# The first attention's output units move into the dilated attention's blocks and are merged there with their gate

## The reference, cut to what matters

```python
proj = rmsnorm(x, g_mix) @ w_in           # q, k, v of both attentions, gate_pre
gates = sigmoid(gate_pre + b_gate)
g_sb, g_dl = gates[..., :1024], gates[..., 1024:]
y_sb = merge_heads(stick_breaking_attention(q_sb, k_sb, v_sb)) @ w_sb_out   # 512 -> 1024
y_dl = merge_heads(dilated_window_attention(q_dl, k_dl, v_dl)) @ w_dil_out  # 256 -> 1024
x = x + (g_sb * y_sb + g_dl * y_dl) @ w_o
```

## Time and profile before

| | us |
|---|---|
| median of 3 runs | 1140.44 (1138.16 to 1141.69) |
| profiled execution | 1136.11 |
| its span, first to last instruction | 1134.3 |
| TensorE busy in the span | 1102.1 (97%), weight load 942.2 (83%) |
| VectorE, ScalarE busy | 769.7 (68%), 540.7 (48%) |
| mean granted TensorE clock | 0.995 of 2.4 GHz |

### The profile page before, as it was taken

One profiled execution on the slowest core, in us unless ns is written; L12 is line 12 of the kernel. 1 busy time (PEld: TensorE's weight loads), 2 busy tenths in 40 slices (PEclk: granted clock), 3 DMA queues, 4 the chain that ended last, 5 costly groups with the idle time before them and its releaser, 6 DMA issues.

```text
span 1134.3 us, 15599 instructions
## 1 busy us (share of the span) xinstructions
PE 1102.1 (97%) x6039; PEld 942.2 (83%) x6039; DVE 769.7 (68%) x1080; ACT 540.7 (48%) x867; POOL 0.2 (0%) x4
## 2 busy tenths in 40 slices
PE   7989999999999999999999999999999999999996
PEld 5888899988998778877677788888898899989985
DVE  6876378745878778677666555568774578637864
ACT  6554155523553466666656433334553355514641
POOL 0000000000000000000000000000000000000000
PEclk9999999999999999999999999999999999999998
DMA  8223233332323212111110133433233233323221
GB/s 285 97 75 113 74 112 112 112 93 93 103 70 125 93 38 72 41 56 50 42 58 29 37 98 95 140 104 93 75 112 112 77 110 111 94 93 112 82 68 75
DMA packets 32904, 102.99 MB, mean 91 GB/s; under 512 B 4160, under 2 KB 5568, under 8 KB 32832
## 3 DMA queue, kind: packets, MB, share of 16 engines
q1 hardware_dynamic: 32832, 102.01, 28.8%
HBM read 99.90 MB, written 2.10 MB: 90 GB/s over the span
## 4 chain that ended last, share of the span: by engine, by line
PE 84%; DVE 8%; ACT 4%; issue 3%; DMA 1%; SPq 0%; DVEq 0%; ACTq 0%
PE acc_pair L1175 24%; PE acc_pair L1177 24%; PE acc_pair L1176 24%; PE pair_bank L1175 2%; PE pair_bank L1176 2%; PE pair_bank L1177 2%; DVE w_lo L758 1%; PE bank L1175 1%; PE bank L1177 1%; PE bank L1176 1%; ACT rope L628 1%; ACT w_hi L471 1%; PE bank L1183 1%; DVE rstd L783 1%; PE bank L1185 1%
## 5 line engine op out<-in xcount | busy, mean ns | idle before, releaser
L1175 PE MATMUL acc_pair<-xg_hi,w_hi 128*128 128x512 f32 (+1 forms) x693 | 266.0, 384 | 7.3 <-DVE w_lo L990 7.3
L1176 PE MATMUL acc_pair<-xg_lo,w_hi 128*128 128x512 f32 (+1 forms) x693 | 260.3, 376 | 0.0
L1177 PE MATMUL acc_pair<-xg_hi,w_lo 128*128 128x512 f32 (+1 forms) x693 | 259.8, 375 | 0.0
L471 ACT ACTIVATE w_hi<-w_raw 128x1024 fp32r<-128x1024 f32 (+2 forms) x159 | 153.5, 976 | 148.8 <-PE acc_pair L1177 148.6
L758 DVE TENSOR_TENSOR w_lo<-w_raw,w_hi 128x1024 fp32r<-128x1024 f32 (+2 forms) x159 | 178.5, 1125 | 46.7 <-ACT w_hi L471 45.3
L1175 PEld LDWEIGHTS acc_pair<-xg_hi,w_hi 128*128 128x128 f32 x693 | 131.2, 189 | 30.7 <-issue 8.0
L1177 PEld LDWEIGHTS acc_pair<-xg_hi,w_lo 128*128 128x128 f32 x693 | 130.8, 189 | 24.6
L1176 PEld LDWEIGHTS acc_pair<-xg_lo,w_hi 128*128 128x128 f32 x693 | 131.4, 190 | 19.9 <-issue 0.7
L1177 PE MATMUL acc_pair<-hid_hi,w_lo 128*128 128x512 f32 x352 | 138.8, 394 | 0.0
L1176 PE MATMUL acc_pair<-hid_lo,w_hi 128*128 128x512 f32 x352 | 138.2, 393 | 0.0
L1175 PE MATMUL acc_pair<-hid_hi,w_hi 128*128 128x512 f32 x352 | 136.9, 389 | 0.0
(11 more groups left out here) (217 smaller groups left out, 2057.6 us busy)
## 6 DMA issues: line engine op xcount, KB each, us to landing
w_raw<-in_w13b SPq DMA_DIRECT2D x44, 512.0 KB, 3.6
w_raw<-in_w13a SPq DMA_DIRECT2D x40, 512.0 KB, 3.8
w_raw<-in_wmix SPq DMA_DIRECT2D x22, 512.0 KB, 3.5
w_raw<-in_w2a SPq DMA_DIRECT2D x16, 512.0 KB, 3.6
w_raw<-in_w2b SPq DMA_DIRECT2D x16, 512.0 KB, 3.5
w_raw<-in_wgate SPq DMA_DIRECT2D x8, 512.0 KB, 3.5
w_raw<-in_wend SPq DMA_DIRECT2D x8, 512.0 KB, 3.4
w_raw<-in_wo SPq DMA_DIRECT2D x8, 512.0 KB, 3.5
```

The costliest lines, as they stand in the source:

```text
L471: act.activation(w_hi[:, s, 0:width], w_raw[:, s, 0:width], ACT.Copy).then_inc(whi_done, 1)
L1175: pe.matmul(o, w_h, r_h, start=first, stop=False, skip_group_check=check)
L1176: pe.matmul(o, w_h, r_l, start=False, stop=False, skip_group_check=check)
L1177: return pe.matmul(o, w_l, r_h, start=False, stop=last, skip_group_check=check)
```

## The change

Each first-attention output unit is put behind its gate unit in the order of units: GATE to END now holds 16 units (gate, output, gate, output, ...), the final loop has two units for each m instead of three. An output unit is 12 matmuls and thus one filler, "Us". It waits for the first attention's result, and is followed by a step "merge": VectorE multiplies the accumulator by (gate + 1) and writes back into the gate's tile. The list has 32 fillers left for the sixteen blocks, and every block gets two; none is left behind the last. `gsb` is moved up in memory by 5000 floats in each partition and its tiles are used from the top down, so that only the tile of m = 7 overlaps the first dilated heads; gates are taken out at once, and only the last waits for the second "dpv".

```diff
-END = GATE + KD
-WO = END + 3 * KD
+END = GATE + 2 * KD
+WO = END + 2 * KD
-DL_FILL = (1, 1, 1, 1, 1, 1, 2, 3, 1, 1, 1, 2, 1, 2, 2, 2)
+DL_FILL = (2,) * 16
-END_COLS = ((0, 1024), (1024, 512), (1536, 256))
+GATE_COLS = ((0, 1024), (1024, 512))
+END_COLS = ((0, 1024), (1024, 256))
...
-    halves = [(half, u) for u in range(MIX, END) for half in ("Ua", "Ub")]
+    halves = [(half, u) for u in range(MIX, END)
+              for half in (("Us",) if u >= GATE and (u - GATE) % 2 else ("Ua", "Ub"))]
...
             if half == "Ub" and u >= GATE:
-                held.append(u)
-        if ("dpv", 1) in s:
-            while held:
-                s.append(("gate", held.pop(0)))
+                s.append(("gate", u))
+            if half == "Us":
+                s.append(("merge", u))
...
-                gsb = sb("gsb", [P, KD, SEQ], F32, att)
+                unused = sb("unused", [P, 5000], F32, att)
+                gsb_tiles = sb("gsb_tiles", [P, KD, SEQ], F32, att)
...
+        def gsb(m):
+            return gsb_tiles[:, KD - 1 - m, :]
...
                 elif kind == "gate":
                     dve.wait_ge(unit_done, w + 1)
-                    dve.wait_ge(pv_done, 2 * SB_PAIRS + 2)
-                    dve.tensor_tensor(gsb[:, w - GATE, :], acc[w % RING][:], rstd[:],
+                    if w == END - 2:
+                        dve.wait_ge(pv_done, 2 * SB_PAIRS + 2)
+                    dve.tensor_tensor(gsb((w - GATE) // 2), acc[w % RING][:], rstd[:],
                                       ALU.mult).then_inc(acc_read[w % RING], 1)
+                elif kind == "merge":
+                    m = (w - GATE) // 2
+                    dve.wait_ge(unit_done, w + 1)
+                    dve.wait_ge(gate_done, m + 1)
+                    dve.scalar_tensor_tensor(gsb(m), gsb(m), 1.0, acc[w % RING][:], ALU.add,
+                                             ALU.mult).then_inc(acc_read[w % RING], 1)
...
-                    elif j % 3 == 1:
+                    else:
+                        dve.wait_ge(gate_done, m + (KD + 1))
+                        dve.scalar_tensor_tensor(part[:, 1, :], gdl[:, j // 2 % 2, :], 1.0, acc[s][:], ALU.add,
+                                                 ALU.mult).then_inc(acc_read[s], 1)
+                        dve.wait_ge(acc_read[s], reads(u, 2 * i) + 1)
                         if m:
                             dve.wait_ge(mg_lo_done, m)
...
+                        dve.tensor_tensor(part[:, 0, :], gsb(m), part[:, 1, :], ALU.add).then_inc(merge_step, 1)
...
+                if kind == "Us":
+                    pe.wait_ge(ys_done, 2 * SB_PAIRS)
+                    unit(w, 0, ys, K8[0:SB_PAIRS])
```

More of the change, by code:

```diff
@@ L91, in unit_width @@
                 return n * P
+    if GATE <= u < END:
+        return GATE_COLS[(u - GATE) % 2][1]
     if END <= u < WO:
-        return END_COLS[(u - END) % 3][1]
+        return END_COLS[(u - END) % 2][1]
     return KD * P
@@ L108, in mix_schedule @@
     s = []
-    held = []
-    halves = [(half, u) for u in range(MIX, END) for half in ("Ua", "Ub")]
+    halves = [(half, u) for u in range(MIX, END)
+              for half in (("Us",) if u >= GATE and (u - GATE) % 2 else ("Ua", "Ub"))]
     def fill(n):
@@ L449, in _ @@
             for u in range(GATE, END):
-                load(u, 0, A["wgate"][u - GATE])
+                c, n = GATE_COLS[(u - GATE) % 2]
+                load(u, 0, A["wgate"][(u - GATE) // 2, :, c:c + n])
             for u in range(END, WO):
-                c, n = END_COLS[(u - END) % 3]
-                load(u, 0, A["wend"][(u - END) // 3, :, c:c + n])
+                c, n = END_COLS[(u - END) % 2]
+                load(u, 0, A["wend"][(u - END) // 2, :, c:c + n])
             with sp.Fori(0, KD // 4) as i:
@@ L617, in _ @@
             for kind, w in MIX_STEPS:
-                if kind == "Ua":
+                if kind in ("Ua", "Us"):
                     split_hi(w + 2, 0, unit_width(w + 2))
@@ L637, in _ @@
                     act.wait_ge(hbias_made, 1)
-                    act.activation(gsb[:, w - GATE, :], gsb[:, w - GATE, :], ACT.Tanh, scale=0.5,
-                                   bias=hbias[:, 0, w - GATE:w - GATE + 1]).then_inc(gate_done, 1)
+                    m = (w - GATE) // 2
+                    act.activation(gsb(m), gsb(m), ACT.Tanh, scale=0.5,
+                                   bias=hbias[:, 0, m:m + 1]).then_inc(gate_done, 1)
                 elif kind == "fin":
@@ L727, in _ @@
             for i in range(KD // 4):
-                for j in range(12):
-                    v = END + 12 * i + j + 2
+                for j in range(8):
+                    v = END + 8 * i + j + 2
                     split_hi(v, 0, unit_width(v))
[L731 to L734, removed]
+                    m = 4 * i + j // 2
+                    if j % 2 == 0:
+                        act.wait_ge(acc_read[(END + j) % RING], reads(END + j, 2 * i) + 1)
+                        act.activation(gdl[:, j // 2 % 2, :], gdl[:, j // 2 % 2, :], ACT.Tanh, scale=0.5,
                                        bias=hbias[:, 1, m:m + 1]).then_inc(gate_done, 1)
-                    if j % 3 == 2:
+                    else:
                         act.wait_ge(merge_step, m + 1)
@@ L1125, in _ @@
             for i in range(KD // 4):
-                for j in range(12):
-                    u, v = END + j, END + 12 * i + j + 2
+                for j in range(8):
+                    u, v = END + j, END + 8 * i + j + 2
                     s = u % RING
-                    m = 4 * i + j // 3
+                    m = 4 * i + j // 2
                     split_lo(v, 0, unit_width(v))
-                    dve.wait_ge(unit_done, 12 * i + (u + 1))
-                    if j % 3 == 0:
-                        dve.tensor_tensor(gdl[:, j // 3 % 2, :], acc[s][:], rstd[:], ALU.mult).then_inc(acc_read[s], 1)
-                    elif j % 3 == 1:
+                    dve.wait_ge(unit_done, 8 * i + (u + 1))
+                    if j % 2 == 0:
+                        dve.tensor_tensor(gdl[:, j // 2 % 2, :], acc[s][:], rstd[:], ALU.mult).then_inc(acc_read[s], 1)
+                    else:
+                        dve.wait_ge(gate_done, m + (KD + 1))
+                        dve.scalar_tensor_tensor(part[:, 1, :], gdl[:, j // 2 % 2, :], 1.0, acc[s][:], ALU.add,
+                                                 ALU.mult).then_inc(acc_read[s], 1)
+                        dve.wait_ge(acc_read[s], reads(u, 2 * i) + 1)
                         if m:
                             dve.wait_ge(mg_lo_done, m)
[L1137 to L1145, removed]
+                        dve.tensor_tensor(part[:, 0, :], gsb(m), part[:, 1, :], ALU.add).then_inc(merge_step, 1)
                         dve.wait_ge(merge_step, m + 1)
@@ L1326, in _ @@
             ffn(FFN_A, 0, 0)
+            ys = lambda k: (ys_hi[:, k, :], ys_lo[:, k, :])
+            yd = lambda k: (yd_hi[:, k, :], yd_lo[:, k, :])
             for kind, w in MIX_STEPS:
-                if kind == "Ua":
+                if kind == "Us":
+                    pe.wait_ge(ys_done, 2 * SB_PAIRS)
+                    unit(w, 0, ys, K8[0:SB_PAIRS])
+                elif kind == "Ua":
                     unit(w, 0, xg, K8, (lambda k: pe.wait_ge(xg_lo_done, KD + k + 1)) if w == MIX else None, half=0)
@@ L1425, in _ @@
                     mm.then_inc(pv_done, 1)
-            ys = lambda k: (ys_hi[:, k, :], ys_lo[:, k, :])
-            yd = lambda k: (yd_hi[:, k, :], yd_lo[:, k, :])
             with pe.Fori(0, KD // 4) as i:
-                for j in range(0, 12, 3):
-                    unit(END + j, 3 * i, xg, K8)
+                for j in range(0, 8, 2):
+                    unit(END + j, 2 * i, xg, K8)
                     if j == 0:
                         pe.wait_ge(ys_done, 2 * (SB_PAIRS + DL_PAIRS))
-                    unit(END + j + 1, 3 * i, ys, K8[0:SB_PAIRS])
-                    unit(END + j + 2, 3 * i, yd, K8[0:DL_PAIRS])
+                    unit(END + j + 1, 2 * i, yd, K8[0:DL_PAIRS])
             for m in range(KD):
@@ L1504 @@
     gate0 = first["rv"] + DL_PAIRS
-    wend = np.concatenate([win[gate0 + KD:gate0 + 2 * KD], units(a["w_sb_out"][0]),
-                           units(a["w_dil_out"][0])], 2)
+    wgate = np.concatenate([win[gate0:gate0 + KD], units(a["w_sb_out"][0])], 2)
+    wend = np.concatenate([win[gate0 + KD:gate0 + 2 * KD], units(a["w_dil_out"][0])], 2)
     cols = lambda v: v.reshape(-1, P).T
@@ L1513 @@
         "w13b": pairs(a["w1_b"][0], a["w3_b"][0]), "w2b": units(a["w2_b"][0]),
-        "wmix": win[order], "wgate": win[gate0:gate0 + KD], "wend": wend, "wo": units(a["w_o"][0]),
+        "wmix": win[order], "wgate": wgate, "wend": wend, "wo": units(a["w_o"][0]),
     }
```

1 line of the change is left out of this document (added).

## The result

Beside each other on one chip the kernel before took 1141.06 us (median of 5 runs) and the changed kernel 1132.92 us (1131.99 to 1133.82): a ratio of 0.9932, 95% interval 0.9917 to 0.9946. Forecast were 1133.9 us in a range of 1129 to 1139, a gain of 6.5 us; measured are 8.1.

A forecast was written before the change was run, and what follows sets the result against it. TensorE, busy 1102.1 of 1134.3 us, was taken to bound the kernel, so only its losses could be won: 11.2 - 3.0 - 1.5 - 0.2 = 6.5 us, taking the median from 1140.4 to 1133.9 us, range 1129 to 1139.

The forecast's parts named there:

- waits and restarts: TensorE in the dilated blocks: ten waits, 8.1 us, plus 0.15 us restart each, 9.6 us to win.
- Two fillers a block: Dilated blocks: scores, transposes and two fillers take TensorE 7.9 us a block, hiding the old waits on exponential and scaling.
- (3): First four blocks: weight split ahead of the sums lengthens the serial loop to 8.9 us; 3.0 us of new waits.
- (4): The twelve later blocks: gates and merges delay the sums without any TensorE wait; cost 0, 2 us of margin.
- (5): Behind the last block no filler is left: last product with the values waits 1.5 us, bounds 0.3 and 2.
- (6): Final loop: 6.88 us a TensorE round, other engines' 6.8 barely fits, cost 0; mg_lo 0.2 us late at the last round.
- The bound of 8 rounds by 0.6 us: Final loop: worst case, given as 4 us, if the removed split had hidden behind ScalarE anyway.
- The clock: Dilated blocks, 527 to 608 us: granted clock 0.98 costs 1.6 us, counted as winnable.
- rival C: Clock falls in two places, first blocks and tail, 1.6 us each: 3.3 us gained, 1137.1 us; chance 0.13.
- The sum: Whole kernel: 11.2 us winnable less 3.0, 1.5 and 0.2 us of new waits, 6.5 us gained.
- From the profile to the median: Whole kernel: profiled 1136.1 us lies 4.3 below the median 1140.4; same difference applied to 1129.6 gives 1133.9 us.

The follow-up runs named there:

- e6: Changed kernel with the second gate's product in each final-loop round made three times on VectorE; 1141.77 us, ratio 0.9996 to the kernel before.
- e7: Changed kernel with each of the eight gate products in the blocks made three times on VectorE; 1134.11 us, ratio 0.9926 to the kernel before.
- e2: Changed kernel with one filler instead of two in the last block, one kept behind it; 1132.31 us, ratio 0.9931 to the kernel before.
- e3: Kernel before with its own 23 fillers placed otherwise, two in each of the first four blocks; 1135.44 us, ratio 0.9954.

## Why the prediction was right

**Where the gain is (waits and restarts, 9.6 us).** Right: all ten waits went. The restart of 0.15 us each was read at one gap, and the sum does not decide it: without the clock's 1.7 us the stretch gained 4.9 us, the waits alone are 8.1 - 3.4 = 4.7, and with restarts 5.6. e6 speaks for them: 6.3 us more of waits and 1.8 for its fall are 8.1, six more restarts make it 9.0, and its stretch grew by 9.3.

**Two fillers a block, 7.9 us.** Right. The transposes of blocks 2 to 4 and of 8 and 9:

```profile
546.79 0.66 PE L1433 MATMUL bank<-identf,prob 128*128 128x128 f32 x4 [1.08 <-ACT prob L724]
555.41 0.66 PE L1433 MATMUL bank<-identf,prob 128*128 128x128 f32 x4 [0.49 <-ACT prob L724]
563.34 0.60 PE L1433 MATMUL bank<-identf,prob 128*128 128x128 f32 x4
...
589.27 0.60 PE L1433 MATMUL bank<-identf,prob 128*128 128x128 f32 x4
597.16 0.60 PE L1433 MATMUL bank<-identf,prob 128*128 128x128 f32 x4
```

8.62 us, then 7.93 and 7.89.

**(3), what is late next.** The mechanism and its place were right, the size was not: 1.5, 1.2 and 0.3 us forecast, 1.08, 0.49 and 0 measured, 3.0 against 1.6 (1.9 with restarts). The loop was 8.61 us where I had 8.9 (ScalarE's timeline after, answering to the earlier trace rows):

```profile
547.08 0.90 ACT L718 ACTIVATE prob<-pair_bank,stats 128x768 f32<-128x768 f32 x1 [0.34 <-DVE stats L1116]
551.21 0.60 ACT L732 ACTIVATE pT_hi<-bank 128x512 fp32r<-128x512 f32 x1
551.70 1.05 ACT L479 ACTIVATE w_hi<-w_raw 128x1024 fp32r<-128x1024 f32 x1
555.69 0.90 ACT L718 ACTIVATE prob<-pair_bank,stats 128x768 f32<-128x768 f32 x1 [0.34 <-DVE stats L1116]
```

w_hi starts 0.49 us behind the start of pT_hi, before pT_hi's 0.60 are over; I had added whole durations and a hand-over. That accounts for 0.2 of the 0.3 us.

**(4), no wait in the gate blocks.** Right that no wait came. e7 shows the margin: 1.35 us more in each cost nothing in blocks 5 to 14 but 0.3 us in block 15, so the 2 us of margin do not hold there. In the last block I had seen the tail but not that its scaling has hardly any margin; e2 and e7 found it.

**(5), the tail.** 1.5 us forecast, 1.46 measured.

**(6), the final loop.** 6.88 us a round forecast; VectorE's gate products start at 671.74 and 678.62, 6.88 apart:

```profile
671.74 0.69 DVE L1149 TENSOR_TENSOR gdl<-acc_pair,rstd 128x512 f32<-128x512 f32 x1 [0.55 <-PE acc_pair L1189]
...
678.62 0.69 DVE L1149 TENSOR_TENSOR gdl<-acc_pair,rstd 128x512 f32<-128x512 f32 x1 [0.46 <-PE acc_pair L1189]
```

The wait for mg_lo was 0.34 us, forecast 0.2. The other engines' loop was oversized: 6.8 us forecast, 6.3 by e6, so the margin was about 0.5 us and not 0.1, which did not touch the sum. (The bound of 8 rounds by 0.6 us is 4.8 us, not the 4 written there.)

**The clock (1.6 us, rival C).** In the stretch it was gained as forecast. I had no ground for saying whether a fall would come back, and falls at other places came in one profile of the changed kernel and not in the other. Rival C had the direction wrong: fewer waits went with a higher clock, 0.9941 against 0.9892 over all timed runs.

**The sum.** 11.2 gone; 3.4 us of new waits and 4 x 0.15 of restarts came: 7.2 us. Measured in the stretch: 6.6. The cause of the missing 0.6 is not shown; a filler is 9.63 - 6.88 = 2.75 us in the final loop and 2.82 with its change-over in a block, which for eight of them would make it, as an estimate. So the forecast's 6.5 for the stretch came out in part by luck: (3) was 1.1 us too large, the tail and mg_lo with their restarts 0.4 too small, and the missing 0.6 hid the rest.

**From the profile to the median.** This step failed, though the time came out. I gave the changed kernel the 4.3 us by which the profiled execution of before lies under its median. That distance was the clock's: the profiled execution had 0.995, the 53 runs 0.9892 in the mean. The changed kernel's profiled execution had 0.992 and took 1133.07 us, as long as its median. At the same clock 4.9 us were forecast (9.6 - 4.7) and 5.0 measured, so the mechanism holds; from the clock 1.6 were forecast, and 4.7 came in the mean of all runs. That the median lies 1.0 us from the forecast is the sum of the two in a comparison where the changed kernel had 0.9932, below its mean.

## What to carry to other kernels

Where one engine is full in one stage and waits in another, moving its work between the stages gains the waits, and here also a higher granted clock; count the waits with their restarts before, and the new serial loops that the moved work enters. An engine's busy share says nothing on such a loop: follow one round of it from instruction to instruction, and for each instruction moved look both at what it stood in front of and at what it will stand in front of. When falls of the clock come and go, compare profiles over a stretch that both kernels have, not by their spans, and timed runs at the same granted clock.

## What I had not expected

A change of 6.6 us in the profiles was 8.1 and 12.2 us in two timed comparisons, about half of it by a higher clock: the kernel before has waits of 0.2 to 2.3 us in the blocks, and in its second profile the clock fell twice among them. And a kernel whose fillers are only placed otherwise (e3) gained 5.0 us of time for one line, 2.7 of them at the same clock, about half of what the change gained in both countings.
